# A hybrid decoder step on one core: where the gates, the sample convolution and the norm sums are computed

## What is computed

```python
proj = xn @ w_in                                    # 1024 -> 6 x 1024
u_x, u_y, c_v, c_g, g_rnn, g_conv = jnp.split(proj, SPLITS, axis=-1)
xc, new_c4 = _causal_dwconv(u_x, c4, rnn_conv_w, rnn_conv_b)             # 4 taps
...
h, h_last = _lru_scan(a, bseq, h0)
rnn_out = (h.astype(xn.dtype) * jax.nn.gelu(u_y)) @ w_rnn_proj
glu = c_v * jax.nn.sigmoid(c_g)
cc, new_c31 = _causal_dwconv(glu, c31, conf_conv_w, conf_conv_b)         # 31 taps
conv_out = jax.nn.silu(_layernorm(cc, conf_ln_g, conf_ln_b)) @ w_conv_proj
merged = jax.nn.sigmoid(g_rnn) * rnn_out + jax.nn.sigmoid(g_conv) * conv_out
return merged @ w_out, h_last, new_c4, new_c31
```

## Time and profile before

| what | value |
|---|---|
| median of 3 runs | 713.68 us (711.88 to 715.61) |
| profiled execution, own time | 713.11 us |
| its span, first to last instruction | 711.3 us |
| mean granted clock of TensorE | 0.943 |
| PE busy | 631.5 us, 89% of the span |
| DVE busy | 548.0 us, 77% |
| ACT busy | 371.8 us, 52% |
| POOL busy | 178.1 us, 25% |

### The profile page before, as it was taken

How to read it: one execution, slowest core, us unless ns; L and a number is a source line. 1 busy time by engine, 2 the same in 40 slices (tenths; PEclk the granted TensorE clock), 3 DMA queues, 4 the chain that set the end, 5 groups by cost and what they waited for, 6 DMA issues and landing times.

```text
span 711.3 us, 8239 instructions
## 1 busy us (share of the span) xinstructions
PE 631.5 (89%) x2972; PEld 475.3 (67%) x2972; DVE 548.0 (77%) x754; ACT 371.8 (52%) x526; POOL 178.1 (25%) x129
## 2 busy tenths in 40 slices
PE   5999999896584978999998999999999999999940
PEld 4677777674584978997777756666666666666620
DVE  2169887899899999875549788888888888888506
ACT  2120103661831422743345887777777777777522
POOL 1019870334395520041000021111111111111110
PEclk8699999999697988999999999999999999999985
DMA  9766063324033150534044689999999999997114
GB/s 266 228 200 237 1 237 119 118 88 148 2 119 118 51 187 3 192 77 178 0 175 182 251 335 354 364 354 370 365 373 368 365 382 364 366 364 297 37 59 158
DMA packets 45718, 150.21 MB, mean 211 GB/s; under 512 B 9990, under 2 KB 13302, under 8 KB 33062
## 3 DMA queue, kind: packets, MB, share of 16 engines
q1 hardware_dynamic: 36000, 144.04, 54.6%
q10 hardware_dynamic: 6086, 3.06, 1.9%
q0 software_dynamic: 3584, 2.50, 1.1%
HBM read 145.51 MB, written 15.02 MB: 226 GB/s over the span
## 4 chain that ended last, share of the span: by engine, by line
PE 56%; DVE 5%; DMA 2%; issue 1%; ACT 1%; SPq 0%; ACTq 0%; POOLq 0%; DVEq 0%
PE bank L1619 25%; PE bank L1644 14%; PE bank L1434 7%; PE bank L1529 5%; PE bank L1586 2%; DMA ring<-expert_rows 1%; PE bank L1631 1%; PE bank L1501 1%; DVE conv L1064 1%; DVE x L1357 1%; DMA expert_rows<-work,row_i 0%; DVE gel_lo L1022 0%; DVE x L1347 0%; PE bank L1491 0%; DVE x L1345 0%
## 5 line engine op out<-in xcount | busy, mean ns | idle before, releaser
L1266 DVE TENSOR_TENSOR lo_gu<-ring,hi_gu 128x2048 fp32r<-128x2048 f32 x64 | 143.8, 2288 | 39.7 <-ACT hi_gu L799 39.7
L1439 PE MATMUL bank<-work,ring 128*128 128x304 f32 x512 | 134.8, 424 | 0.9 <-ACT work L581 0.9
L954 DVE SCALAR_TENSOR_TENSOR work<-work,par 128x272 f32<-128x272 f32 x240 | 131.6, 621 | 0.0
L1439 PEld LDWEIGHTS bank<-work,ring 128*128 128x128 f32 x512 | 98.4, 193 | 35.4 <-issue 2.4
L799 ACT ACTIVATE hi_gu<-ring 128x2048 fp32r<-128x2048 f32 x64 | 118.6, 1902 | 0.0
L1619 PE MATMUL bank<-hi_gu,xe_hi 128*96 128x512 f32 x256 | 102.4, 400 | 0.6 <-ACT work L823 0.6
L1619 PE MATMUL bank<-hi_gu,xe_lo 128*96 128x512 f32 x256 | 100.5, 393 | 0.0
L1619 PE MATMUL bank<-lo_gu,xe_hi 128*96 128x512 f32 x256 | 100.4, 392 | 0.0
L1434 PE MATMUL bank<-xn_hi,w_hi 128*128 128x304 f32 x128 | 41.6, 325 | 26.9 <-DVE xn_lo L1022 15.0
L1644 PE MATMUL bank<-ring,windows 128*96 128x512 f32 x128 | 65.2, 590 | 0.0
L528 POOL DMA_INDIRECT expert_rows<-outst,row_i x16 | 25.6, 1602 | 157.9 <-ACT outst L817 157.9
(11 more groups left out here) (279 smaller groups left out, 1188.1 us busy)
## 6 DMA issues: line engine op xcount, KB each, us to landing
ring<-w_exp_gate SPq DMA_DIRECT2D x32, 1024.0 KB, 6.9
ring<-w_exp_up SPq DMA_DIRECT2D x32, 1024.0 KB, 9.6
ring<-w_exp_down SPq DMA_DIRECT2D x32, 1024.0 KB, 10.0
ring<-w_in SPq DMA_DIRECT2D x11, 2048.0 KB, 8.2
ring<-w_rnn_proj SPq DMA_DIRECT2D x2, 2048.0 KB, 7.9
ring<-w_conv_proj SPq DMA_DIRECT2D x2, 2048.0 KB, 8.4
ring<-w_out SPq DMA_DIRECT2D x2, 2048.0 KB, 8.1
ring<-w_in SPq DMA_DIRECT2D x2, 1024.0 KB, 11.0
```

Of the source, the lines that this page charges most:

```text
L954: ins = vec.scalar_tensor_tensor(y, glu[:, ch, w:w + TP], pcw[:, w, ch:ch + 1], y, ALU.mult, ALU.add)
L1266: vec.tensor_tensor(part, whole, as_f32(high), ALU.subtract).then_inc(out_done, 1)
L1439: ins = mm(bank[m % 4][:, 0:T], mix_w[b % MIX_SLOTS][:, i, (c % MB) * P:(c % MB + 1) * P], xnT[:, i], start=(i == 0), stop=(i == KT - 1))
```

## The change

Four things change, and what hangs on them moves along.

The gate: ACT no longer copies `cv`. DVE multiplies the `cv` bank with the sigmoid of `cg` (`gate`), so that a `cv` bank is free when DVE is done with it (`glu_done`). Tap 0 of the prompt convolution goes from DVE to ACT (`first_tap`).

The samples: the new columns of `glu` are set to zero at first. `old_samples` multiplies and sums the windows on DVE, now with stored rows alone, before they are needed; `new_samples` adds bias and the four diagonals of new columns for all channels at once. The stored rows must be there early: `crow` becomes the fourth load of ACT's queue, PE turns it before `xn`, and the banks for turning `xn` become 2, 3, 0, 1. The gate weights are loaded by SP after block 3.

The norm: the two reduces on DVE are gone. PE adds the eight channel tiles by eight products each; centering and squaring go in two halves.

`gr` and `gc` become plain float32 tiles. 12 units remain, all low halves on DVE; `xn` has no halves any more. The gates of the recurrence come three tiles later between the tiles (`ux` 5 to `uy` 4), and DVE's list is written anew.

```diff
-        first_split, first_tile = blocks.index(("gr", 0)), tile_at["gr", 0]
+        first_split, first_tile = blocks.index(("rp", 0)), tile_at["rp", 0]
...
             for b in range(NBLK):
                 load_block(b)
+                if b == MIX_SLOTS - 1:
+                    sp.wait_ge(zeros, 1)
...
-            for c in range(KT):
-                pool.wait_ge(tile_act, 2 * c + 2)
-                nc.gpsimd.tensor_tensor(glu[:, c, CW - 1:GLP], cv_sb[:, c % 2, 0:TP], sg_sb[:, c % 2, 0:TP], ALU.mult)
...
             act.dma_start(prow[0:64, 3], a["state_rglru_h"][0].rearrange("s (c p) -> (s c) p", p=P)).then_inc(par_in, 16)
+            act.dma_start(crow[0:120], a["state_conformer_conv"][0].rearrange("s r (c p) -> (s r c) p", p=P)
+                          .rearrange("(i q) p -> q i p", i=16)).then_inc(cst_in, 16)
...
+            def first_tap(c):
+
+                act.wait_ge(glu_done, c + 1)
+                nc.scalar.activation(cc[:, c, 0:TP], glu[:, c, 0:TP], ACT.Identity, scale=pcw[:, 0, c:c + 1],
+                                     bias=pccb[:, c:c + 1]).then_inc(tap0_done, 1)
...
+            def gate(c):
+
+                m = tile_at["cv", c]
+                dve.wait_ge(tile_act, evacuated(m + 1))
+                vec.tensor_tensor(glu[:, c, CW - 1:GLP], bank[m % 4][:, 0:TP], sg_sb[:, c % 2, 0:TP], ALU.mult)
...
+            def old_samples(c):
+
+                g = glu[:, c, GLP:GLN].rearrange("p (s j) -> p s j", s=NS)
+                if c:
+                    dve.wait_ge(cstep, 2 * c)
+                for t in range(TS):
+                    ins = vec.tensor_tensor(win4[:, :, t, :], g[:, :, t:t + CW],
+                                            pcw[:, :, c].unsqueeze(1).broadcast_to([P, NS, CW]), ALU.mult)
+                ins.then_inc(cstep, 1)
+                dve.wait_ge(cstep, 2 * c + 1)
+                vec.tensor_reduce(cc[:, c, TP:T], win.rearrange("p (n w) -> p n w", w=CW), AX_X, ALU.add).then_inc(cstep, 1)
...
+            for c in range(3):
+                old_samples(c)
+            gate(0)
+            for c in range(3, 6):
+                old_samples(c)
+            gate(1)
+            conv_prompts(0, between={4: lambda: old_samples(6), 5: lambda: gate(2), 10: lambda: old_samples(7),
+                                     13: lambda: gate(3), 22: lambda: gate(4)})
+            conv_prompts(2, between={1: lambda: gate(5), 10: lambda: gate(6), 18: lambda: gate(7), 24: new_samples})
...
+            conv_prompts(6, between={12: lambda: weight_low(0), 18: lambda: weight_low(1), 24: lambda: weight_low(2)})
...
-            dve.wait_ge(conv_done, KT)
-            vec.tensor_reduce(csum, cc.rearrange("p c n -> p n c"), AX_X, ALU.add).then_inc(sum_done, 1)
...
                 if m >= 4:
-                    if m - 4 < NACT:
-                        pe.wait_ge(tile_act, m - 3)
+                    if tiles[m - 4][0] == "cv":
+                        pe.wait_ge(glu_done, tiles[m - 4][1] + 1)
+                    elif m - 4 < NACT:
+                        pe.wait_ge(tile_act, evacuated(m - 4))
...
                 if (k, c) == ("rp", 1):
-                    pe.wait_ge(sum_done, 1)
                     pe.wait_ge(st_ev, 2)
-                    mm(bank[4][:, 0:T], ones_d, csum, start=True, stop=True).then_inc(mean_mm, 1)
+                    pe.wait_ge(smp_done, 1 + 2 * TS)
+                    for i in range(KT):
+                        pe.wait_ge(tap_done[i % 2], (i // 2 + 1) * (CW - 1))
+                        ins = mm(bank[4][:, 0:T], ones_d, cc[:, i], start=(i == 0), stop=(i == KT - 1))
+                    ins.then_inc(mean_mm, 1)
```

More of the change, by code:

```diff
@@ L47 @@
 EXP_SLOTS = 4
-POOL_UNITS = (3, 5, 7)
+TURNED_BANKS = (2, 3, 0, 1)
 HI_SLOTS = 3
@@ L915, in _ @@
                             bank[1][:, 0:192].rearrange("p (s r c) -> p s r c", s=NS, r=RW - 1)).then_inc(rst_done, 1)
+            for s in range(NS):
+                dve.wait_ge(cst_T, s // 2 + 1)
+                at = GLP + s * GLS
+                b = bank[4 + s // 2][:, 240 * (s % 2):240 * (s % 2) + 240]
+                vec.tensor_copy(glu[:, :, at:at + CW - 1], b.rearrange("p (r c) -> p c r", c=KT)).then_inc(cst_done, 1)
             dve.wait_ge(par_done, 1)
@@ new lines, in new_samples @@
+            def new_samples():
+                step = Steps(dve, smp_done)
+                y = cc[:, :, TP:T].rearrange("p c (s t) -> p c s t", s=NS)
+                step(vec.tensor_tensor(cc[:, :, TP:T], cc[:, :, TP:T], pccb.unsqueeze(2).broadcast_to([P, KT, NS * TS]), ALU.add))
+                dve.wait_ge(glu_done, KT)
+                for d in range(TS):
+                    n = TS - d
+                    prod = smp[:, 0:KT * NS * n].rearrange("p (c s t) -> p c s t", c=KT, s=NS)
+                    tap = pcw[:, CW - 1 - d].unsqueeze(2).unsqueeze(3).broadcast_to([P, KT, NS, n])
+                    step(vec.tensor_tensor(prod, new_glu[:, :, :, 0:n], tap, ALU.mult))
+                    step(vec.tensor_tensor(y[:, :, :, d:], y[:, :, :, d:], prod, ALU.add))
@@ L947, in conv_prompts @@
+            def conv_prompts(c, taps=range(1, CW), between=None):
                 for w in taps:
@@ L1074, in _ @@
             vec.tensor_copy(outst[:, 7 * P:9 * P], bank[6][:, 2 * P:4 * P]).then_inc(st_ev, 1)
-            weight_low(9)
+            tile("rp", 0)
             dve.wait_ge(mean_mm, 1)
-            vec.tensor_tensor(cc, cc, bank[4][:, 0:T].unsqueeze(1).broadcast_to([P, KT, T]), ALU.subtract)\
-               .then_inc(cen_done, 1)
-            tile("rp", 0)
-            weight_low(10)
+            for q in range(2):
+                half = slice(q * HB, q * HB + HB)
+                vec.tensor_tensor(cc[:, half], cc[:, half], bank[4][:, 0:T].unsqueeze(1).broadcast_to([P, HB, T]), ALU.subtract)\
+                   .then_inc(cen_done, 1)
             tile("rp", 1)
-            dve.wait_ge(sq_done, 1)
-            vec.tensor_reduce(csum, sq.rearrange("p c n -> p n c"), AX_X, ALU.add).then_inc(sum_done, 1)
+            weight_low(3)
             tile("rp", 2)
-            weight_low(11)
             tile("rp", 3)
@@ L1392, in conf_states @@
                 ins.then_inc(cst_T, 1)
+            pe.wait_ge(cst_in, 16)
+            for g in range(4):
+                conf_states(g)
             pe.wait_ge(xn_done, NT)
             for j in range(KT):
+                if j == 2:
+                    pe.wait_ge(par_done, 1)
+                    pe.wait_ge(rst_done, 1)
                 if j >= 4:
@@ L1427, in tile @@
                     x_hi, x_lo, ready = {"rp": (rows(gel_hi), rows(gel_lo), glo_done),
-                                         "cp": (rows(cc_hi), rows(cc_lo), clo_done)}.get(k, (xn_hi, rows(xn_lo), xlo_done))
+                                         "cp": (rows(cc_hi), rows(cc_lo), clo_done)}[k]
                     cols = slice((c % 2) * P, (c % 2 + 1) * P)
```

236 lines of the change are left out of this document (86 added, 150 removed).

## The result

The changed kernel takes **702.55 us** (median of 4, 701.98 to 702.84) where the kernel before takes 712.88 beside it (711.88 to 715.61): ratio 0.9848, 95% interval 0.9818 to 0.9878. That is 10.3 us faster, inside the range and 1.5 us under the forecast of 704. The profiled execution took 702.46 us, its span is 700.6.

What follows compares the result with a forecast made beforehand. The prediction took DVE, with POOL's late low halves, to bound the mixer up to 262.7 us and PE from there. Terms +9.4 - 22.7 + 4.1 = -9.2 on a 711.3 us span, plus 1.8, gave 704 us; range 695 to 716.

Steps and rivals of the forecast that it cites:

- The first tile at 36.7: Start of PE's first plain tile, forecast 11.8 us later than before because the conv states are turned before xn.
- I take 24: Start: the early conv states land at 24 us, between 17.4 at the earliest and 25 at the latest.
- +8.0 as before: Start: PE's turning of xn before the first tile takes 8.0 us, as in the kernel before.
- the rival of early states: Start: states land at 17.4, first tile at 30.1, time 697.5 us; chance 0.13.
- Products at 0.34: DVE's window products in the conv samples: 0.34 us each.
- stalls of 1.5: Plain tiles up to uy: 1.5 us charged for PE waiting on DVE's gates.
- The rival: DVE cannot feed PE: window products at POOL's 0.90 us each, PE waits 13 us longer, time 717; chance 0.13.
- The turning point of 0.77: Window products on DVE: at about 0.77 us each, no gain from the change is left.
- `uy` at 180.1: End of the last uy tile on PE: 180.1 us instead of 170.75, +9.4.
- Piece two, 69.3: From the end of uy to the first rp product, gr and gc plain: 69.3 us instead of 92.0, -22.7.
- Piece three, 65.3: From rp to wo, with norm sums on PE: 65.3 us instead of 61.2, +4.1.
- The rival of the norm as bound: Norm sums between rp tiles take 8.2 us each instead of 4.1, time 712; chance 0.14, shared with several small slips.

Runs made afterwards that it cites:

- e1: The changed kernel with the conv states' load last in ACT's queue and their turns on PE behind those of xn: 697.04 us.
- e5: The changed kernel with the window products' taps copied once into contiguous rows by channel: 702.09 us.
- e2: e1 with the states' turns behind the third tile and whole windows multiplied on DVE only after the gates: 694.35 us.
- e4: The changed kernel with one of its two norm sums, that of squares, back on DVE as a reduce: 698.63 us.
- e10: e2 with both norm sums as DVE reduces, three windows in DVE's idle gaps, later low halves, and contiguous taps as in e5: 685.55 us.

## Why the prediction was right, and where not

*The first tile at 36.7.* Measured 36.65, by two errors that cancel. "I take 24" for the landing was 26.96, 3.0 late; I counted with the states and not with the load of recurrence states two places behind them. "+8.0 as before" for turning `xn` took 5.4 (31.23 to 36.65), for the granted clock is 0.50, the lower of its two levels, while PE turns parameters and states (26.96 to 31.23), and 1.00 over the turns of `xn`. That the two come to the same size is luck. Before, those turns came first behind the idle time and had the lower level. I had taken the slow clock for a property of the start; the rows tie it to the work that comes first behind an idle PE. The Trainium skill ("DMA: Bandwidth & Descriptors", Specifications) gives 512 bytes as enough for line rate, from which the prediction estimated some 3 us for the states; they landed 23.0 us after issue beside x and the first weight blocks, and 24.0 in e1 with the queue in another order. That estimate does not agree with the trace, and the rival of early states falls; how fast such pieces are with nothing beside them no run shows.

*Products at 0.34, stalls of 1.5.* Both were too low: 0.54, and 2.7 us at gates. So one sign of being wrong, PE waiting for `gate`, came true, though the sum itself had 1.5 us of it. The rival had priced a product of 0.51 from the strided reduce, and I took the contiguous one. (That 0.51 is 0.34 scaled by 1.8 to 1.2; 248 words at 1.8 ns are 0.45, under the measured 0.54 too.) With contiguous taps it is 0.35 (e5): my 0.34 was the price of an operand that the code does not have. The 16-byte-line rule of the Trainium skill ("SBUF — State Buffer", Door 1) points the way that these rows went; it has no size. The turning point of 0.77 was not reached.

*`uy` at 180.1.* Measured 179.85 (the row of tiles that begins at 167.56, three of which are `uy`). The longer stalls are made good by the first tiles, which run at the high level from the start: six in 24.80 us, 4.13 each, against 14.61/3 = 4.87 before. So "a start at the slow clock, which both kernels have" was wrong, and that this covers the stalls is luck again.

*Piece two, 69.3.* Measured 69.56, with a wait of 2.93 for 2.8 and 19.76 us of idle DVE for 20. Right step by step. What it did not ask is what those 20 us were for. The sum set the start (+9.4) and the tail (+4.1) against the plain tiles (-22.7) as parts of one whole, and let DVE's relief stand on the gaining side. The plain tiles alone gain 29.7: the rest of the change costs 18.7 more than it brings. From the rows: first tile 36.65 against 24.98, +11.7; from there to `rp` 212.8 against 213.7, -0.9; `rp` to `wo` 65.3 against 56.9, +8.4; 19.2 in all. DVE got room that it had no use for, and PE, the bound by then, paid for it. The experiments undo it piece by piece: e1 5.5 us, e2 (with e1 in it) 8.2, e4 3.9, and with the remaining waits and the taps in rows 17.0 together (e10).

*Piece three, 65.3.* Measured 65.34: sums of 4.09 (4.1), `rp` 0 at 5.13 (5.0); `cc_lo` held PE 0.6 us and some gaps more (1.6). The rival of the norm as bound needed half clock at the sums; the granted clock from 249.4 to 280 is 0.94 on average and 0.67 only within `rp` 0.

*The sum.* The three pieces measured +9.1, -22.4 and +4.1, -9.2 in all as forecast. The 1.5 us by which the time lies under 704 are behind the start of `wo`, where the prediction put no difference. They are one row of 12 `wo` products, before and after:

```profile
356.88 4.51 PE bank L1529 x12
```

```profile
347.72 2.98 PE bank L1517 x12
```

The granted clock over it is 0.63 before and 1.00 after. The same row takes 2.98 with the plain tiles alone and 4.54 in e10, so it does not go with the change; what decides it stays open.

## What to carry over

When a part of a change moves the bound to another engine, cost the other parts against the new bound: run the part that carries the gain alone. Work that is taken from an engine with idle time gained next to nothing here, and what it cost on the bound showed in full (e4). And an engine's queue is part of the price: a first tap that is cheap behind a gate on DVE held all of ACT behind a gate on POOL.

## What the hardware showed that I had not expected

- A 4 KB load took 7.37 us to issue, and the next 3.11, with 960 KB in pieces of 512 bytes ahead of them in ACT's queue; with the same load last, issuing the three took 0.50, 0.38 and 0.47 us (ACT's timeline of e1).
- A 248-word product on DVE took 0.54 us with its second operand one word in eight and 0.35 with the operand contiguous.
- 12.2 us of work on POOL lengthened DVE's taps beside it by 8.5 us; the other way, beside 46 taps of DVE in a row one POOL product, 0.76 us otherwise, lasted 19.56 (19.03 in the earlier trace rows).
- After a wait of 2.9 us the granted clock over the first `rp` tile was 0.67 in one kernel and 0.52 in another, 1.24 us apart: enough to swallow half of a gain of 2.5 us.

Two kernels are the fastest of all, equal within their intervals: the plain tiles alone, 683.86 us, with the smaller edit, and e10, 685.55.
